# Two fused transformer blocks in three-product float32: the feature products done as three matmuls of 256 columns into one PSUM range instead of one of 512 and one of 256

## The reference, cut to what matters

```python
# first block
z = rmsnorm(x) @ w_in                    # conv (cb, cc, cv), q, k, v, f, two gates
conv_branch = (cb * causal_dwconv(cc * cv)) @ w_conv_out
attn_branch = forgetting_attention(q, k, v, log_f) @ w_attn_out
x = x + (gc * conv_branch + ga * attn_branch) @ w_mix_out
x = x + square(relu(rmsnorm(x) @ w_ff1)) @ w_ff2
x = rmsnorm(x)
# second block
q, k, v, p = split(rms_norm(x) @ w_in_2)
x = x + concat(moba_attention(q, k, v), multiscale_pool(p)) @ w_out_2
x = x + conv_ffn(rms_norm(x))            # w_up_2 (gate and value), w_down_2
```

## Time and profile before

| | before |
|---|---|
| median of three runs | 2383.57 us |
| the profiled execution: its time | 2383.46 us |
| its span, first to last instruction | 2381.6 us |
| TensorE matmul busy | 2376.9 us, 100% |
| TensorE weight load busy | 2035.4 us, 85% |
| VectorE busy | 1700.7 us, 71% |
| ScalarE busy | 1216.5 us, 51% |
| DMA engines, mean | some 60%, 190 GB/s |

### The profile page before, as it was taken

How to read it: one execution, slowest core, us unless ns; L and a number is a source line. 1 busy time by engine, 2 the same in 40 slices (tenths; PEclk the granted TensorE clock), 3 DMA queues, 4 the chain that set the end, 5 groups by cost and what they waited for, 6 DMA issues and landing times.

```text
span 2381.6 us, 30785 instructions
## 1 busy us (share of the span) xinstructions
PE 2376.9 (100%) x12581; PEld 2035.4 (85%) x12581; DVE 1700.7 (71%) x1804; ACT 1216.5 (51%) x1427; POOL 0.2 (0%) x4
## 2 busy tenths in 40 slices
PE   9999999999999999999999999999999999999999
PEld 8888888888888888888888888888888888888887
DVE  6565666666568868868768667855778778886788
ACT  5444454554545445445445555555555455545554
POOL 0000000000000000000000000000000000000000
PEclk9999999999999999999999999999999999999999
DMA  7566556666555665655665565555655665566655
GB/s 253 160 187 196 167 185 196 191 188 196 186 187 178 219 216 189 213 181 198 202 190 193 182 185 160 171 183 186 186 181 194 196 192 176 186 219 186 188 173 181
DMA packets 238040, 452.15 MB, mean 190 GB/s; under 512 B 16569, under 2 KB 20779, under 8 KB 237771
## 3 DMA queue, kind: packets, MB, share of 16 engines
q1 hardware_dynamic: 237147, 449.07, 59.3%
q10 hardware_dynamic: 752, 1.12, 0.1%
HBM read 446.46 MB, written 3.67 MB: 189 GB/s over the span
## 4 chain that ended last, share of the span: by engine, by line
PE 97%; DVE 2%; ACT 0%; issue 0%; ACTq 0%; DVEq 0%
PE PS L684 41%; PE PS L686 21%; PE PS L717 11%; PE PS L718 11%; PE PS L719 11%; DVE WL L1279 1%; PE PS L648 0%; PE PS L615 0%; PE PS L636 0%; PE PS L657 0%; ACT WH L840 0%; PE PS L542 0%; PE PS L625 0%; DVE PB L1259 0%; PE PS L553 0%
## 5 line engine op out<-in xcount | busy, mean ns | idle before, releaser
L1279 DVE TENSOR_TENSOR WL<-RAW,WH 128x1024 fp32r<-128x1024 f32 (+1 forms) x844 | 1002.0, 1204 | 520.6 <-ACT WH L840 519.1
L684 PE MATMUL PS<-XHL,WH 128*128 128x512 f32 x3968 | 1248.9, 396 | 0.0
L840 ACT ACTIVATE WH<-RAW 128x1024 fp32r<-128x1024 f32 (+1 forms) x845 | 867.5, 1041 | 744.4 <-PE PS L686 478.3
L686 PEld LDWEIGHTS PS<-XHL,WL 128*128 128x128 f32 x3968 | 745.4, 188 | 176.0
L686 PE MATMUL PS<-XHL,WL 128*128 128x256 f32 x3968 | 779.7, 278 | 0.0
L684 PEld LDWEIGHTS PS<-XHL,WH 128*128 128x128 f32 x3968 | 605.1, 189 | 2.1 <-issue 1.0
L717 PE MATMUL PS<-WH,MHL 128*128 128x512 f32 x1000 | 390.2, 390 | 0.0
L719 PE MATMUL PS<-WH,MHL 128*128 128x512 f32 x1000 | 389.2, 389 | 0.0
L718 PE MATMUL PS<-WL,MHL 128*128 128x512 f32 x1000 | 389.1, 389 | 0.0
L719 PEld LDWEIGHTS PS<-WH,MHL 128*128 128x128 f32 x1000 | 187.7, 188 | 39.3
L717 PEld LDWEIGHTS PS<-WH,MHL 128*128 128x128 f32 x1000 | 187.7, 188 | 38.8 <-issue 0.3
(11 more groups left out here) (212 smaller groups left out, 1374.6 us busy)
## 6 DMA issues: line engine op xcount, KB each, us to landing
RAW<-in_w_ff SPq DMA_DIRECT2D x256, 512.0 KB, 4.1
RAW<-in_w_in SPq DMA_DIRECT2D x224, 512.0 KB, 3.9
RAW<-in_w_up SPq DMA_DIRECT2D x176, 512.0 KB, 4.1
RAW<-in_w_down SPq DMA_DIRECT2D x88, 512.0 KB, 4.4
RAW<-in_w_mix_out SPq DMA_DIRECT2D x32, 512.0 KB, 4.0
RAW<-in_w_out SPq DMA_DIRECT2D x32, 512.0 KB, 3.7
RAW<-in_w_conv_out SPq DMA_DIRECT2D x16, 512.0 KB, 3.7
RAW<-in_w_attn_out SPq DMA_DIRECT2D x16, 512.0 KB, 4.3
```

The lines of the kernel that those rows point to most:

```text
L684: mm(PS[:, b + p.banks[j], :], h[:, k, j * P:(j + 1) * P], x[:, kc, :], start=st, stop=False)
L686: t = mm(PS[:, b + p.banks[j], 0:T], l[:, k, j * P:(j + 1) * P], x[:, kc, 0:T], start=False, stop=en)
L840: act(high, raw, AF.Copy).then_inc(*own.made(hi, i))
L1279: tt(low, raw, high.bitcast(f32), sub).then_inc(*own.made(lo, i))
```

## The change

A step of a feature item becomes six matmuls of 256 columns: `WH` of both tiles against the high columns, `WL` of both against the high columns, `WH` of both against the low columns. All three products of a tile are added into the same 256 PSUM columns. Two tiles share a bank, so an item takes two banks (the "front" of its side), and the other two (the "back") serve the small products. The folds are gone: what comes after them reads PSUM itself (`product(it)`, `four(bank)`).

```diff
-                        for j0 in range(0, len(p.banks), 2):
-                            for j in (j0, j0 + 1):
-                                mm(PS[:, b + p.banks[j], :], h[:, k, j * P:(j + 1) * P], x[:, kc, :], start=st, stop=False)
-                            for j in (j0, j0 + 1):
-                                t = mm(PS[:, b + p.banks[j], 0:T], l[:, k, j * P:(j + 1) * P], x[:, kc, 0:T],
-                                       start=False, stop=en)
+                        for pair in range(0, len(p.quarters), 2):
+                            two = [(h[:, k, j * P:(j + 1) * P], l[:, k, j * P:(j + 1) * P],
+                                    PS[:, b + p.quarters[j] // 2, T * (j % 2):T * (j % 2) + T]) for j in (pair, pair + 1)]
+                            for j, (wh, _, o) in enumerate(two):
+                                mm(o, wh, x[:, kc, 0:T], start=st and j == 0, stop=False)
+                            for _, wl, o in two:
+                                mm(o, wl, x[:, kc, 0:T], start=False, stop=False)
+                            for j, (wh, _, o) in enumerate(two):
+                                t = mm(o, wh, x[:, kc, T:2 * T], start=False, stop=en and j == 1)
...
-            def fold(it):
-                own.wait_ge(*used[it.end])
-                if free["TA"]:
-                    s, key = free["TA"]
-                    own.wait_ge(*s[key])
-                chain()
-                e.copy(TA[:], wide_ps(it, T, 2 * T)).then_inc(*own.made(copied, it.key))
-                yield
...
-            def fold(it):
-                chain()
-                own.wait_ge(*copied[it.key])
-                tt(TA[:], TA[:], wide_ps(it, 0, T), add).then_inc(*own.made(left, it.key))
-                yield
...
+            def product(it):
+                chain()
+                own.wait_ge(*used[it.end])
+                return four(it.bank)
+
+            def scale_rows(it):
+                tt(TA[:], product(it), over4(RB[:]), mul).then_inc(*own.made(left, it.key))
...
-                tt(TB[:, :, 0:T], TA[:], over4(RB[:]), mul).then_inc(*own.made(evacuated, it.key))
+                tt(TB[:, :, 0:T], product(it), over4(RB[:]), mul).then_inc(*own.made(evacuated, it.key))
```

More of the change, by code:

```diff
@@ L531, in tensor, with front_of, back_of, all_of @@
             mm, transpose = e.matmul, e.transpose
[L533 to L537, removed]
+            front, back = [None, None], [None, None]
+            def front_of(s):
+                if front[s]:
+                    own.wait_ge(*front[s][0][front[s][1]])
                 return 4 * s
+            def back_of(s):
+                if back[s]:
+                    own.wait_ge(*back[s][0][back[s][1]])
+                return 4 * s + 2
+            def all_of(s):
+                back_of(s)
+                return front_of(s)
             def zeros(n):
@@ L556, in first @@
                 if u == 7:
-                    free[1] = x_lo, ("mix", 15)
+                    front[1] = back[1] = x_lo, ("mix", 15)
             def vec(s):
-                b = take(s)
+                b = back_of(s)
                 own.wait_ge(s_const, 16)
@@ L579, in spread @@
                 t.then_inc(*own.made(spread_up, key))
-                free[s] = row, key
+                back[s] = row, key
             def log_f(s):
-                b = take(s)
+                b = back_of(s)
                 own.wait_ge(*evacuated["f"])
@@ L617, in score @@
                 t.then_inc(*own.made(scores, (block, h)))
-                free[s] = masked, (block, h)
+                front[s] = back[s] = masked, (block, h)
             def turn(s, block, h):
-                b = take(s)
+                b = all_of(s)
                 own.wait_ge(*normed["P", block, h])
@@ L762, in group @@
                     if c:
-                        free[it.side ^ 1] = left, it.key
+                        front[it.side ^ 1] = back[it.side ^ 1] = left, it.key
                 last = {"out": (stored, (it.args["g"], 1, 1)), "final group": (evacuated, ("final", 1))}
-                free[it.side] = last.get(it.kind, (evacuated, it.key))
+                front[it.side] = back[it.side] = last.get(it.kind, (evacuated, it.key))
             own.wait_ge(*zero_made["zero"])
@@ L1048, in ff @@
             def ff(it):
-                yield from fold(it)
+                yield from fresh(it)
                 yield from nothing(2)
@@ L1086, in qk @@
             def qk(it):
-                yield from fold(it)
-                free["TA"] = evacuated, it.key
+                yield from fresh(it)
                 yield
@@ L1116, in pool @@
             def pool(it):
[L1117 removed]
                 chain()
+                may_write_ta()
                 own.wait_ge(*multiplied[it.key])
@@ L1201, in parts @@
                             work.flush()
-                            g = pooled(args[0])
-                            next(g)
-                            work.later(g)
+                            work.later(pooled(args[0]))
             free["EV"] = None
@@ L1522, in cb @@
             def cb(it):
-                yield from fold(it)
-                scale_rows(scaled, it.key)
+                scale_rows(it)
                 yield
@@ L1531, in gates @@
             def gates(it):
-                yield from fold(it)
-                scale_rows(scaled, it.key)
+                if it.args["half"]:
+                    own.wait_ge(*gate["gc", it.args["g"]])
+                scale_rows(it)
                 yield
@@ L1670, in qk @@
             def qk(it):
-                yield from fold(it)
+                yield from fresh(it)
                 dst, c0 = (Q2 if it.key[0] == "Q" else K2), it.args["c0"]
-                chain()
-                stt(dst[:, c0:c0 + 4, :], TA[:], 1.0, over4(RB[:]), mul, mul).then_inc(*own.made(evacuated, it.key))
+                stt(dst[:, c0:c0 + 4, :], product(it), 1.0, over4(RB[:]), mul, mul).then_inc(*own.made(evacuated, it.key))
                 yield
@@ L1697, in pool @@
             def pool(it):
-                yield from fold(it)
                 i = it.args["i"]
-                chain()
-                tt(TC[:, :, 16:272], TA[:], over4(RB[:]), mul).then_inc(*own.made(multiplied, it.key))
+                tt(TC[:, :, 16:272], product(it), over4(RB[:]), mul).then_inc(*own.made(multiplied, it.key))
                 e.memset(TB[:, :, 0:16], 0.0).then_inc(*own.made())
@@ L1750, in up_gate @@
                     e.memset(TC[:, :, 0:2], 0.0).then_inc(*own.made())
-                yield from fold(it)
-                chain()
-                tt(TC[:, :, 2:258], TA[:], over4(RB[:]), mul).then_inc(*own.made(multiplied, it.key))
+                yield from fresh(it)
+                tt(TC[:, :, 2:258], product(it), over4(RB[:]), mul).then_inc(*own.made(multiplied, it.key))
                 yield
```

227 lines of the change are left out of this document (107 added, 120 removed).

## The result

The changed kernel takes 2438.84 us (median of 4 runs, 2438.0 to 2439.39) where the kernel before takes 2383.55 (4 runs). The ratio is 1.0231, 95% interval 1.0213 to 1.0248: 55 us slower. The span of the profiled execution went from 2381.6 to 2436.9 us.

What follows compares the result with a forecast made beforehand. The prediction took TensorE's queue of matmuls as the bound: 2120 feature steps going from 0.697 to 0.727 us add 64 us to 2383.46, removed work and waits nothing, giving 2447 us; forecast's own range 2432 to 2456, overall 2384 to 2462.

Steps and rivals of the forecast that it cites:

- What bounds: Whole kernel: a queue of TensorE matmuls with 1.0 us of waits; work removed from ScalarE and VectorE gains nothing.
- The mechanism: Feature steps: six matmuls for four over the same 1536 columns cost more, as each matmul has its own price.
- fixed part: Every matmul: time over its columns, 13 to 14 ns from the earlier trace, taken as 14.5 ns with six.
- The size of the step: Feature step: from 0.697 us to 0.727 with six matmuls, bounds 0.720 to 0.731, over 2120 steps.
- The waits: TensorE's waits stay near 1 us; VectorE's new wait for TensorE when first reading a product costs nothing.
- The reading of the earlier trace: Token item after a feature item: its first six matmuls repay about 0.03 us that short matmuls seemed to save.
- Rival B: Feature steps: cost goes mostly with columns, step 0.699 us, 4 us slower, 2388 us (2384 to 2400); chance 0.17.
- Rival C: Feature steps: short matmuls are cheaper, six make 0.690 us, 15 us faster, 2369 us; chance 0.13.
- Rival D: Feature steps: weight loads or issue become the bound; at 0.13 us a load, 176 us slower, 2559 us; chance 0.08.

Runs made afterwards that it cites:

- e1: Kernel before, with each 512-column matmul in token items and groups issued as two of 256 with the same stationary block; 2431.46 us, ratio 1.0201.
- e2: Changed kernel loading only 64 of 128 stationary columns in feature items, except first and last input blocks, leaving out part of the sum; 2369.65 us.
- e5b: Changed kernel loading only 32 of 128 stationary columns in feature items, except first and last input blocks, leaving out part of the sum; 2414.53 us.
- e4: Kernel before, with a feature step's four matmuls alternating long and short (512, 256, 512, 256 columns); 2392.49 us, ratio 1.0043.
- e3: Changed kernel with the empty piece left by the fold put back at the head of the up value items' evacuation; 2432.12 us, ratio 1.0205.
- e8b: Kernel before, with an entry's 16 matmuls sorted by length, eight of 512 columns, then eight of 256; 2386.86 us, ratio 1.0015.
- e6b: Changed kernel with each 256-column matmul in feature items issued as two of 128, twelve a step; 3748.56 us.
- e7b: Kernel before with each fold's work doubled: ScalarE copies twice, VectorE adds a multiply by 1.0; 2403.69 us, ratio 1.0086.
- e10: Kernel before in alternating order, plus one extra short matmul before the first of feature items following a token item or group; 2396.38 us, ratio 1.0053.

## Why the prediction was right, and where it was off

- *What bounds.* Right. A queue of matmuls with next to no waits, so the time follows the step. The 84 us (I had said 88) and 74 us that VectorE and ScalarE lost bought nothing.
- *The mechanism.* Right as far as it was put as a price that comes again with each matmul, its load included: more matmuls for the same columns cost more, on both sides of the array (e1). What the price is made of I had left as "a fixed part" of the matmul's issue. That is not borne out: with narrower stationary tiles it changes (e2), and at one width it differs between stretches (e2, e5b). With full tiles of 128 columns the changed kernel has 0.120 a matmul in every long feature stretch of its trace. What makes it stays open.
- *The size of the step.* I took 0.727 us, with 0.720 to 0.731 as bounds; measured 0.720, my lower bound. The term that was mis-sized is the fixed part with six matmuls, 14.5 ns; it is 13.3, as in the token items. I had carried on from three matmuls (13.3) to four (14.2) to six. But the 0.9 ns more belong to the mixture of long and short matmuls, not to their number: with six of one length they are gone, and with the same four in another order the step is 0.693 in some stretches and 0.707 in others (e4). This made my sum 15 us too high.
- *The waits.* I put them at nothing; they were 5 us, from the order of pieces and not from VectorE's new wait for TensorE, as e3 shows. It is a cost of taking something away that I had not looked for. The two errors offset each other in part: 2447 predicted, 2438.84 measured, within the range of the forecast (2432 to 2456). That the waits brought the time nearer to 2447 is luck; without them (e3) it is 2432, at the lower bound.
- *The reading of the earlier trace rows.* Wrong, though it pointed the right way. I took the 0.03 us that the first long matmuls of a token item lose for a debt that the short ones had run up by starting ahead. The changed kernel loses the same there:

```profile
586.42 0.40 PE L740 MATMUL PS<-WH,MHL 128*128 128x512 f32 x1
...
587.81 0.39 PE L740 MATMUL PS<-WH,MHL 128*128 128x512 f32 x1
```

1.39 us for six, behind short matmuls that were already 0.120 apart, with no lead. And e8b loses it at each entry. It is a price of going from short to long; what makes it is not shown.
- *Rival B* (cost by columns) fell with the step of 0.720. Its premise, that a matmul of 512 columns costs 0.232 because it moves `XHL`, fell with e8b: the last of eight such matmuls are 0.227 apart. Item `f`, on which it rested, loads 16 columns only; that its 0.232 comes from the narrow load is likely by e5b, but not tested. *Rival C* fell: six in a row don't keep the 0.115 of two. *Rival D* fell: a long run of loads at 0.12 us holds, and even at 0.112 (e6b).

## What to carry to other kernels

Where matmuls fill the span, count the matmuls as well as their columns: each one of this kind, with 128 stationary columns of fp32r, cost 13.3 ns over its columns, and splitting one of 512 in two costs that once more. Taking 158 us of work off engines that wait for TensorE won nothing; putting some 100 us more on them cost 20 (e7b), so read the waits and not the busy time. And when a piece of an interleaved order is removed, look at what moves up into its place: here that cost 5 us, a tenth of the 49 of the steps.

## What the runs showed of the hardware

- The usual surcharge of a matmul of 256 columns changes with the stationary columns, but not in proportion: 13.3 ns for 128, 9.3 for 96, 6.7 for 64, 11.1 for 32. In other stretches 64 columns had the 13.3 of 128, and 32 had the 6.7 of 64. Why is open, as is the question whether the time goes in the load or in the write to PSUM. The 2.5 ns over the columns that the Trainium skill gives for the gap of a single warm matmul ("TensorE: Matmul & The Clock Gate", Back-to-back issue gap) are not seen in any of these fp32r streams.
- The same alternating instructions ran at 0.693 us a step in some stretches and 0.707 in others, each kind stable for up to hundreds of steps. Where I looked, the kind changed at the start of an item or behind a small gap; what sets it is not shown, and I found no way to choose it (e10).
- After a settled run of short matmuls the next five or so long ones are slower, some 28 ns in all, in e8b at each entry.
